# The second layer's last projection in seven half-size products, and the row additions of the down projection in another order

## The reference, cut to what matters

```python
# first layer, feed-forward
hid = silu(hn @ w_ffn_gate) * (hn @ w_ffn_up)      # [512, 2816]
x = x + hid @ w_ffn_down                            # "down", 2816 x 1024
x = rmsnorm(x, norm_final_g)
# second layer
a   = (attention(...) * silu(za)) @ w_att_out
sgo = (spatial_gating(...) * silu(zs)) @ w_sg_out   # 1024 x 1024
y = ga * a + gs * sgo                               # [512, 1024]
x = x + y @ w_o                                     # "wo", 1024 x 1024
return rmsnorm(x, final_g)
```

## Time and profile before

| | us |
|---|---|
| median of 3 runs | 1275.97 |
| profiled execution, its own time | 1276.38 |
| its span, first to last instruction | 1274.6 |
| PE busy | 1253.1 (98%) |
| DVE busy | 776.6 (61%) |
| ACT busy | 539.1 (42%) |
| POOL busy | 130.1 (10%) |
| share of the last chain of work on PE | 89% |

### The profile page before, as it was taken

One profiled execution on the slowest core, in us unless ns is written; L12 is line 12 of the kernel. 1 busy time (PEld: TensorE's weight loads), 2 busy tenths in 40 slices (PEclk: granted clock), 3 DMA queues, 4 the chain that ended last, 5 costly groups with the idle time before them and its releaser, 6 DMA issues.

```text
span 1274.6 us, 15492 instructions
## 1 busy us (share of the span) xinstructions
PE 1253.1 (98%) x6066; PEld 1050.5 (82%) x6066; DVE 776.6 (61%) x1220; ACT 539.1 (42%) x948; POOL 130.1 (10%) x193
## 2 busy tenths in 40 slices
PE   9999999999999999999999899999999999999997
PEld 8878888888888888888888688878888888888886
DVE  6885677653645555565666469858875436436554
ACT  5456665642334333333322353438763343223233
POOL 0002250220000100100000000005550000000000
PEclk9999999999999999999999999999999999999999
DMA  6241323123533943782332223321105322322221
GB/s 198 65 113 61 84 75 92 51 83 99 177 105 112 248 135 99 234 194 99 99 133 99 82 67 116 111 87 34 55 13 168 113 88 78 110 89 99 85 97 66
DMA packets 112820, 134.34 MB, mean 105 GB/s; under 512 B 14118, under 2 KB 89964, under 8 KB 112748
## 3 DMA queue, kind: packets, MB, share of 16 engines
q1 hardware_dynamic: 105820, 116.58, 28.5%
q0 software_dynamic: 6912, 16.78, 5.9%
q10 hardware_dynamic: 16, 0.00, 0.0%
HBM read 128.10 MB, written 2.10 MB: 102 GB/s over the span
## 4 chain that ended last, share of the span: by engine, by line
PE 89%; DVE 5%; ACT 3%; issue 1%; POOL 1%; DMA 0%; SPq 0%; ACTq 0%; DVEq 0%
PE ps_mm L2153 57%; PE ps_mm L2188 16%; PE ps_s L2469 3%; PE ps_s L2314 1%; DVE w_lo L1325 1%; PE ps_t L2469 1%; PE ps_o L2469 1%; ACT w_hi L784 1%; PE ps_o L2345 1%; PE ps_mm L2228 1%; PE ps_o L2587 1%; PE ps_s L2367 1%; PE ps_t L2325 1%; PE ps_o L2394 1%; PE ps_t L2574 1%
## 5 line engine op out<-in xcount | busy, mean ns | idle before, releaser
L2153 PE MATMUL ps_mm<-act_hi,w_hi 128*128 128x512 f32 x944 | 372.4, 394 | 1.1 <-DVE w_lo L1325 1.1
L2153 PE MATMUL ps_mm<-act_hi,w_lo 128*128 128x512 f32 x944 | 370.0, 392 | 0.0
L2153 PE MATMUL ps_mm<-act_lo,w_hi 128*128 128x512 f32 x944 | 369.8, 392 | 0.0
L1325 DVE TENSOR_TENSOR w_lo<-stage,w_hi 128x2048 fp32r<-128x2048 f32 (+5 forms) x99 | 207.5, 2096 | 157.5 <-ACT w_hi L784 157.3
L784 ACT ACTIVATE w_hi<-stage 128x2048 fp32r<-128x2048 f32 (+5 forms) x100 | 173.7, 1737 | 153.3 <-PE ps_mm L2153 66.5
L2153 PEld LDWEIGHTS ps_mm<-act_hi,w_hi 128*128 128x128 f32 x944 | 177.4, 188 | 37.4 <-DVE w_lo L1325 2.6
L2153 PEld LDWEIGHTS ps_mm<-act_hi,w_lo 128*128 128x128 f32 x944 | 177.4, 188 | 35.8
L2153 PEld LDWEIGHTS ps_mm<-act_lo,w_hi 128*128 128x128 f32 x944 | 177.5, 188 | 34.4
L2188 PE MATMUL ps_mm<-w_hi,act_hi 128*128 128x512 f32 (+2 forms) x208 | 77.6, 373 | 0.6 <-DVE lat L1455 0.5
L2188 PE MATMUL ps_mm<-w_lo,act_hi 128*128 128x512 f32 (+2 forms) x208 | 77.1, 370 | 0.0
L2188 PE MATMUL ps_mm<-w_hi,act_lo 128*128 128x512 f32 (+2 forms) x208 | 77.0, 370 | 0.0
(11 more groups left out here) (439 smaller groups left out, 2194.3 us busy)
## 6 DMA issues: line engine op xcount, KB each, us to landing
stage<-in_w_in SPq DMA_DIRECT2D x43, 1024.0 KB, 5.2
sums<-in_w_ffn_down POOLq DMA_DIRECT2D x16, 1024.0 KB, 9.5
stage<-in_w_ffn_gate SPq DMA_DIRECT2D x11, 1024.0 KB, 5.8
stage<-in_w_ffn_up SPq DMA_DIRECT2D x11, 1024.0 KB, 7.0
stage<-in_w_ffn_down SPq DMA_DIRECT2D x8, 1024.0 KB, 5.0
stage<-in_w_out SPq DMA_DIRECT2D x4, 1024.0 KB, 5.5
stage<-in_w_att_out SPq DMA_DIRECT2D x4, 1024.0 KB, 5.2
stage<-in_w_sg_out SPq DMA_DIRECT2D x4, 1024.0 KB, 5.4
```

Source lines behind the costliest of these rows:

```text
L1325: V.tensor_tensor(w_lo[:, s, 0:k * w], raw, w_hi[:, s, 0:k * w].bitcast(F32), ALU.subtract).then_inc(w_lo_made, 1)
L2153: ins = T.matmul(ps_mm[:, 2 * bank_slot + m, :], wt[:, kk, m * P:(m + 1) * P], acts[ap][:, kk, :], start=(r == 0), stop=(r == per - 1), sk ...
```

## The change

**In "down"**, DVE's four row additions of the first half come before it splits the weights of unit 3, and the gain multiplications stay behind that.

**"wo" becomes seven products** P1, P2, P6, P7, P4, P5, P3 of 24 matmuls each (168 in place of 192). In each, two token halves j = 0, 1 of 12 matmuls. P1, P2, P3 take plain quarters of `w_o`. P6, P7 and P4 take sums, which POOL's adding loads build in `tsum`; P5's sum is built in the stage slot of P2 once that is free. The activation sums S1 to S4 come from DVE (`row_sums`), are rounded by ACT (`sy_hi`) and split by DVE (`sums_lo`), all during "sgo". P1's result is copied by ACT (`p1_y`) and added by DVE to three blocks (`spread`). Half of the gain multiplications go to POOL. Token tiles are finished in the order 2, 3, 0, 1. The load of `final_g` moves to the four constant loads before "u2" unit 2.

The core of the diff (other lines only rename or index by group name):

```diff
-          ("sgo", 4), ("wo", 4)]
+          ("sgo", 4), ("wo", 7)]
+SUM_LOADS = {"prod0": 0, "prod1": 8, "wo": 16}
+SUM_WHOLE = {..., "wo": {"P7": 4, "P6": 5, "P4": 6}}
+ORDER = {n: PRODUCTS if n.startswith("prod") else ("P1", "P2", "P6", "P7", "P4", "P5", "P3") for n in GROUPED}
+STAGED = {U0["wo"] + ORDER["wo"].index("P5")}
+FIN_ORDER = (2, 3, 0, 1)
...
# SP
-                if u == U0["wo"]:
-                    sp.wait_ge(vs_normed, TT)
-                    sp.dma_start(lng_b[:, :], A["final_g_2"]...)
+                if u == U0["u2"] + 2:
+                    sp.dma_start(final_g, A["final_g_2"]...)
+            u = U0["wo"]
+            straight(u)
+            straight(u + 1)
+            sp.wait_ge(w_lo_made, u + 1)
+            load(u + 6, u % 2, *unit_source(u + 6))
...
# POOL
+            n, loads = "wo", SUM_LOADS["wo"]
+            u5 = unit_of(n, "P5")
+            pool.wait_ge(mix_gated, 8)
+            for i in range(2):
+                block_into(tsum[:, i, :], sum_landed, n, 0, 1)
+            pool.wait_ge(sum_landed, 16 * (loads + 2))
+            for i in range(2):
+                block_into(tsum[:, i, :], sum_landed, n, 1, 1, add=True)
+            pool.wait_ge(sum_landed, 16 * (loads + 4))
+            block_into(tsum[:, 0, :], sum_landed, n, 0, 0, add=True)
+            pool.wait_ge(w_lo_made, unit_of(n, "P2") + 1)
+            block_into(stage[:, u5 % 2, :], staged_landed, n, 0, 0)
+            pool.wait_ge(staged_landed, 16)
+            block_into(stage[:, u5 % 2, :], staged_landed, n, 0, 1, add=True)
+            pool.wait_ge(w_lo_made, unit_of(n, "P6") + 1)
+            pool.wait_ge(sum_landed, 16 * (loads + 5))
+            block_into(tsum[:, 0, :], sum_landed, n, 1, 0, add=True)
+            pool.wait_ge(fg_landed, 16)
+            for p, half, tiles in (("P2", 0, (0, 1)), ("P4", 0, (2, 3)), ("P5", 1, (2, 3))):
+                for j, t in enumerate(tiles):
+                    pool.wait_ge(product_kept, kept_at(n, p) + j + 1)
+                    G.tensor_tensor(gained(t, half), res[:, t, cc], final_g[:, cc], ALU.mult).then_inc(row_gained, 1)
...
# ACT, in the loop over the sgo units, behind hi(u + 1) and the two act_hi
+                    if c == KD - 1:
+                        hi(U0["wo"] + 1)
...
+                act.wait_ge(s_summed, 4 * GROUPS + i + 1)
+                nc.scalar.activation(sy_hi[:, i, :, :]..., tmp[:, :, :]..., ACT.Copy).then_inc(op_hi_made, 1)
...
# DVE, down
-            def down_rows(n):
+            def down_rows(n, tokens):
+            def down_gains(n, tokens=slice(0, TT)):
...
             lo(ud + 1)
             lo(ud + 2)
+            down_rows(0, slice(0, TT))
             lo(ud + 3)
-            down_rows(0)
+            down_gains(0)
             lo(ud + 4)
...
# DVE, sgo and wo
+            def row_sums(i):
+                even, odd, a, b = gu[:, 2 * i, :], gu[:, 2 * i + 1, :], slice(0, 2 * P), slice(2 * P, S)
+                dve.wait_ge(y_sum, 2 * i + 2)
+                if i:
+                    dve.wait_ge(op_made, 4 * GROUPS + i)
+                link(V.tensor_tensor(tmp[:, 1, a], even[:, a], even[:, b], ALU.subtract))
+                after(link(V.tensor_tensor(tmp[:, 0, a], even[:, b], odd[:, b], ALU.subtract)))
+                after(link(V.tensor_tensor(tmp[:, 0, b], tmp[:, 0, a], even[:, a], ALU.subtract)))
+                V.tensor_tensor(tmp[:, 1, b], odd[:, a], tmp[:, 0, b], ALU.add).then_inc(s_summed, 1)
...
             for i in range(4):
                 u = U0["sgo"] + i
                 lo(u + 1)
+                if i:
+                    sums_lo(i - 1)
...
+                row_sums(i)
+            lo(U0["wo"] + 1)
+            chunk_lo(KD - 1)
+            sums_lo(3)
...
+            lo(u + 2)
+            keep_product("wo", "P2")
+            lo(u + 3)
+            keep_product("wo", "P6")
+            spread(down, left, ALU.add)
+            lo(u + 4)
+            keep_product("wo", "P7")
+            spread(down, right, ALU.subtract)
+            lo(u + 5)
+            keep_product("wo", "P4")
+            spread(up, right, ALU.subtract)
+            lo(u + 6)
+            keep_product("wo", "P5")
...
+            fin_norm(2)
+            fin_norm(3)
+            keep_product("wo", "P3")
...
# PE, product(u)
+                        if n == "wo" and p in ("P1", "P2"):
+                            pe.wait_ge(chunk_lo_made, Y_AT + 2 * kk + (1 if p == "P1" else 2))
+                        else:
+                            pe.wait_ge(op_made, 4 * GROUPED.index(n) + kk + 1)
```

More of the change, by code:

```diff
@@ L116, in group_behind @@
     return {4: 0, 8: 1}.get(j)
[L121 removed]
+WIDE = {"lat": 2, "mv": 1, "dv": 2, "out": 2, "down": 2, "vs": 2}
 GROUP, PLACE, FULL = [], [], {}
@@ L466, in build, with quarter, raw_sum @@
         C2 = {"q2": 0, "kv2": 1024, "za": 1280, "u2": 2304, "vs": 3328, "zs": 4352, "ga": 5376, "gs": 6400}
-        def down_block(g, half, side):
-            return w_down[:, 8 * g + half:8 * g + 8:2, 512 * side:512 * side + 512]
+        def quarter(n, half, side):
+            m, k0 = (wo2, 0) if n == "wo" else (w_down, 8 * int(n[-1]))
+            return m[:, k0 + half:k0 + 8:2, 512 * side:512 * side + 512]
+        def raw_sum(u):
+            n, p = PRODUCT[u]
+            return stage[:, u % 2, :] if u in STAGED else (tsum if n == "wo" else sums)[:, SUM_SLOT[n][p], :]
         def unit_source(u):
@@ L617, in _ @@
                 straight(u)
-            for u in range(U0["q2"], NU):
+            for u in range(U0["q2"], U0["wo"]):
                 if u == U0["za"] + 1:
@@ L716, in _, with block_into @@
                         pool.wait_ge(diff_rstd_made, hd + 1)
[L720 to L724 removed]
+            def block_into(out, signal, n, half, side, add=False):
+                out = out.rearrange("p (k n) -> p k n", k=4)
+                (pool.dma_start(out, quarter(n, half, side), accum_op=ALU.add) if add else
+                 pool.dma_start(out, quarter(n, half, side))).then_inc(signal, 16)
@@ L1849, in _ @@
                 norm_lo_chunk("norm_g_2", 2 * KD, k)
-            down_rows(1)
+            for t in range(TT):
+                down_rows(1, slice(t, t + 1))
+                down_gains(1, slice(t, t + 1))
             for k in range(4, KD):
@@ new lines, in fin_norm, with spread @@
+                dve.wait_ge(row_gained, t + 3) if t >= 2 else dve.wait_ge(x_gained, 8 + t + 1)
+                V.tensor_scalar(res[:, t, D // 2:D], gained(t, 1), y, None, ALU.mult).then_inc(fin_made, 1)
+            def spread(tt, cc, op):
+                link(V.tensor_tensor(res[:, tt, cc], res[:, tt, cc], p1_y[:, :, :], op))
+                after(chain[0])
+            u, right, left, up, down = U0["wo"], slice(512, D), slice(0, 512), slice(0, 2), slice(2, 4)
+            lo(u + 2)
+            keep_product("wo", "P2")
@@ L2110, in _ @@
+            V.tensor_scalar(var[:, 0:4], part[:, 0:4], 1.0 / D, EPS, ALU.mult, ALU.add).then_inc(pre_made, 1)
+            dve.wait_ge(pre_made, 1)
+            fin_norm(2)
+            fin_norm(3)
+            keep_product("wo", "P3")
+            for t in range(2):
+                dve.wait_ge(product_kept, kept_at("wo", "P3") + t + 1)
+                V.tensor_tensor(gained(t, 1), res[:, t, right], final_g[:, right], ALU.mult).then_inc(x_gained, 1)
+                fin_norm(t)
         @block.tensor
```

225 lines of the change are left out of this document (121 added, 104 removed).

## The result

| | before | after |
|---|---|---|
| median, us | 1276.29 (4 runs, 1275.56 to 1276.72) | 1289.32 (4 runs, 1287.62 to 1292.10) |
| profiled execution, its own time | 1276.38 | 1287.62 |
| its span | 1274.6 | 1285.5 |
| PE busy | 1253.1 | 1248.6 |
| mean granted clock of the runs, share of full | 0.998 | 0.997, 0.995, 0.995, 0.993 |

The changed kernel is slower: ratio 1.0106, 95% interval 1.0092 to 1.0120, that is +13.5 us (11.7 to 15.3). The profiled executions differ by 11.2 us in their own time and by 10.9 in their span. PE is busy 4.5 us less and ends later: what was added is waiting.

A forecast was written before the change was run, and what follows sets the result against it. PE is busy nearly all the time, so only its waits and matmul count matter. Terms -4.4 - 5.4 + 8.5 + 7.3 + 1.6 + 1.1 + 2.2 + 0.2 = +11.1 gave 1287.1 us; 8-in-10 range 1279 to 1292.5.

The forecast's parts named there:

- down projection: Unit 2's start: 5.1 us wait and 1.6 us of low clock go, two short waits come; gain 4.4 of 6.7.
- four waits in "sgo", P1, P2: PE waits 1.5 at sgo unit 3, 2.5 at P1, 1.8 at P1's last quarter, 2.6 at P2: together +8.5 us.
- wait before P4: Before P4, PE stands from 1254.7 until its weights are ready at 1262.1: +7.3 us, bounds 2.2 and 11.
- lower clock behind P4's wait: After P4's long wait PE runs at a lower clock, as in the down projection: +1.6 us.
- P3: P3's weights stand in ACT behind the squares of P4's rows, 6.6 against 5.44 us: +1.1 us.
- finish: After PE's last matmul: four token tiles finished one after another, tail 5.7 us where it was 3.4: +2.2.
- starting again: PE's cost of starting again after a wait: +0.2 us.
- The loop of helpers: During "sgo", DVE and ACT hand work round in a 13.40 us turn, 2.5 more than PE's unit of 10.88.
- P4's sum: P4's last adding load queues behind P5's, which needs P2's weights split (1237.6); the sum is whole at 1257.2.
- beside waits for weights: In "wo", POOL's multiplications and the `spread` additions were said to lie beside waits for weights; no cost was given.
- some 11.1 us from P3's start: Finishing four token tiles takes some 11.1 us from P3's start, of which P3 covers 5.44.
- Rival D: PE's clock falls behind four short waits too, up to 6.4 us more, 1291 to 1293.5 us; chance 12%.

The follow-up runs named there:

- the experiment on ACT's order: Changed kernel with ACT's rounding of row sums put behind its rounding of the next weights during "sgo" (units 0 to 2): 1281.54 us, ratio 1.0046.
- the experiment that takes only this away: Changed kernel with POOL's first two multiplications by the gain held until DVE has split P7's weights: 1290.58 us, ratio 1.0113.
- all three edits: Changed kernel with ACT's row-sum rounding later, P4's adding load ahead of P5's, and POOL's first two multiplications held until P7's weights are split: 1275.25 us, ratio 0.9989.
- the last kernel: Changed kernel with all the reorderings tried (ACT, DVE, loads, POOL, finish), plus POOL's pair behind P4 held until P3's weights are split: 1271.09 us, ratio 0.9952.

## Why the prediction was right, point by point

1287.1 us was forecast, 1289.32 measured, 1287.62 in the profiled execution. In us, each as the prediction named it:

| step | forecast | trace after |
|---|---|---|
| down projection | -4.4 | -4.4 (5.56 less 1.2 of the start) |
| 24 matmuls fewer | -5.4 | -5.4 |
| four waits in "sgo", P1, P2 | +8.5 | +8.2 (1.41 + 2.21 + 1.48 + 2.48, and 0.16 each) |
| wait before P4 | +7.3 | +4.7 |
| wait before P7 | 0 | +2.4 |
| lower clock behind P4's wait | +1.6 | +1.5 |
| P3 | +1.1 | +1.3 |
| finish | +2.2 | +3.0 |
| starting again | +0.2 | +0.5 |
| first loads, by chance | 0 | -1.2 |
| sum | +11.1 | +10.6, the spans differ by 10.9 |

(A wait counts here from the start of the matmul before it, less 0.23, so 0.1 to 0.2 more than its idle time.) That the sums agree to 0.5 us is in part luck: the early start (-1.2) makes up for the finish (+0.8) and the slower starts (+0.3), and the wait before P7, which I had at nothing, was taken out of the one before P4. The waits of the third line add up to 8.4 in the prediction's own numbers, not 8.5.

**The loop of helpers.** 13.40 us a turn forecast, 13.38 measured, and the experiment on ACT's order shows that the chain makes it. Adding up DVE's own list would have said that there is room (some 10.5 of 10.88 us, its two short waits for ACT's chunks included), which is true and no help.

**P4's sum.** Forecast whole at 1257.2 on the clock of before, 5.6 less is 1251.6, and it was 1251.6. Missed was the wait before P7: I had put POOL's multiplications "beside waits for weights" at no price. They stand beside a row of DVE with two inputs in SBUF, `w_lo` from `tsum` and `w_hi`, and that row lasted 4.95 us in place of 2.29. Here it cost nothing, shown by the experiment that takes only this away. With the sum landing in time the wait before P7 was 1.67 us, and with POOL held back as well (all three edits) it was gone. The Trainium skill ("SBUF — State Buffer", SBUF: two separate sides) has the rule that I should have set against that sentence: a DVE instruction with two SBUF inputs and a GpSimd instruction that reads SBUF take turns for a shared pair of ports, and the loser stands still. The traces agree in size: DVE's row was 2.66 us longer and POOL's pair ran on for 2.79 us of it (1240.77 to 1243.56). They fit it also where DVE was not slowed: the two additions that read one input from PSUM (0.68 and 0.69 at 1255.35 and 1256.51 in the last kernel) ran beside POOL's pair at their usual length.

**The finish** was 0.8 short. The step that failed is "some 11.1 us from P3's start": it was 12.1, since DVE's rows at 1270.71 and 1271.64 took 0.89 and 1.21 us, and such rows take 0.16 elsewhere, while POOL multiplied from 1270.28 to 1272.83. POOL's pair is the cause again: with these multiplications on DVE the row that stood at 1270.71 takes 0.16 and 0.15, and 0.96 in the last kernel, where another pair of POOL runs beside it. That the rule on two inputs explains it is not shown, since this row has one. No run took this pair of POOL's away and left the rest of the finish as it was. The two rows were 1.8 us longer and the finish only 1.0, so the estimate was 0.8 too long elsewhere.

**The clock.** Rival D had 12%: a lower clock behind short waits too. My argument against it was void: a digit of the page's clock line stands for 32 us, and the digit over the stretch of 0.57 is a 9 as well. Read over 2 us each, the clock behind the 1.4 us wait of before was indeed 1.00. D came true in part. Behind the two short waits of the down projection the clock fell in six of eleven profiled executions, and cost 1.6 us. Behind the waits of 2.2 us before P1 it fell in two of four, and cost nothing, because the next waits took it up. The profiled execution of the changed kernel shows neither. So the forecast for one execution was right, and what I took for the median, 0.4 under the profiled execution as before, was wrong: it lies 1.7 above.

The runs of the changed kernel spread over 4.5 us (1287.62 to 1292.10) while those of before stay within 1.2. The profiles of close variants show where as much can come from. The start moves by 1.5 us, the clock in the down projection costs 1.6, and the lower clock behind P4's wait costs 1.5 here, 2.8 with ACT's other order and 2.6 with POOL held back, each over 24 matmuls. Which of these the three other executions had is not known, since they left no trace. Their mean clock (0.995, 0.995, 0.993) does not tell it. The mean also counts stretches in which PE has nothing left to do:

```profile
1280.00:1284.00 4.00, 0.00 (x0) 0.00 (x0) 1.49 (x7) 1.52 (x4) 0.00 (x0) 0.50 0.50 203
```

And the four runs of the seven products alone have 0.989, 0.990, 0.990 and 0.994 and lie within 1.5 us.

By the Trainium skill ("TensorE: Matmul & The Clock Gate", A second HAM failure mode) frequent micro-idles make the clock go down and up; by these traces they do so in some executions of a program and not in others.

## What to carry to other kernels

Where two helper engines hand work to each other, follow the hand-overs round once and compare the turn with the time of the engine they feed; their busy shares don't tell. Of transfers in one queue, issue first what is needed first: the order of two lines was worth 6 us. Removing 5.4 us of matmuls gained nothing while the waits that the new scheme brought stood, and with nearly all of them gone the gain over the down order alone is still not clear of the noise. Each wait was found by asking what the next one is once this one goes. And read the clock over a few us: a digit for 32 us shows no fall of 4 us.

## What the hardware showed unexpectedly

- **Rows of DVE and POOL.** `w_lo<-tsum,w_hi` 128x2048 took 2.29 us alone and 4.95, 5.07, 4.36 and 4.93 beside two POOL multiplications of 128x512, which took 3.6 us in place of 2.54. Even rows of 128x1 and 128x4 took 1.21 and 0.89 in place of 0.16. Additions of 128x512 with one input in PSUM took their usual 0.7.
- **The same wait, two clocks.** Behind 1.4 and 0.7 us of idle time in the down projection the granted clock was 1.00 in one execution and 0.59 over 4 us in another of the same program, 1.6 us apart. A change that adds short waits can add spread, not only time.
- **Adding loads** of 1 MB from one queue, issued 0.8 us apart: 8.1 us for the first and 12.4 for the second, 8.3 and 12.7 with the two exchanged (8.1 where one was alone).
